# Query rotation moved to GpSimd, its root and the outputs' low halves placed elsewhere in the order

## What is computed

```python
q = rms_norm(q, q_norm); k = rms_norm(k, k_norm)
q = apply_rope(q, cos, sin)      # [t1*cos - t2*sin, t2*cos + t1*sin]
...
scores = einsum('bnqhgd,bnkhd->bnhgqk', qb, kw) * scale
m = maximum(max(scores), sink)
p = exp(scores - m)
probs = p / (sum(p) + exp(sink - m))
out = einsum('bnhgqk,bnkhd->bnqhgd', probs, vw) @ w_o
```

## Time and profile before

| | |
|---|---|
| median of 3 runs | 2738.38 us (2737.41 to 2740.35) |
| the profiled execution's own time | 2737.57 us |
| its span | 2736.3 us |
| PE busy | 2704.9 us |
| DVE, ACT, POOL busy | 1683.6, 1366.9, 0.2 us |
| mean granted clock of PE | 0.998 of full speed |
| HBM read | 491.17 MB |

### The profile page before, as it was taken

The page is one execution under the profiler, slowest core; times in us unless marked ns, Lnnn a source line. Parts: engine busy times, 40 slices in busy tenths (PEclk is TensorE's granted clock), DMA queues, the critical chain, the costliest instruction groups (busy, mean ns, idle before and its releaser), DMA issues.

```text
span 2736.3 us, 34678 instructions
## 1 busy us (share of the span) xinstructions
PE 2704.9 (99%) x13940; PEld 2297.8 (84%) x13940; DVE 1683.6 (62%) x2421; ACT 1366.9 (50%) x2032; POOL 0.2 (0%) x4
## 2 busy tenths in 40 slices
PE   8989999999999999999999999999999999999998
PEld 7768888888888888888888888888888888888886
DVE  6766566556655664565555655544568756785675
ACT  6665544344434455445444644444455535553554
POOL 0000000000000000000000000000000000000000
PEclk9999999999999999999999999999999999999999
DMA  7334666656666577668696555544556565656554
GB/s 235 116 101 154 184 188 188 198 184 193 188 195 191 181 185 198 157 150 181 188 194 221 172 184 187 191 146 157 186 178 207 182 207 179 198 184 202 185 185 146
DMA packets 256994, 495.54 MB, mean 181 GB/s; under 512 B 17201, under 2 KB 18481, under 8 KB 256322
## 3 DMA queue, kind: packets, MB, share of 16 engines
q1 hardware_dynamic: 256834, 493.33, 59.4%
HBM read 491.17 MB, written 2.10 MB: 180 GB/s over the span
## 4 chain that ended last, share of the span: by engine, by line
PE 96%; ACT 2%; DVE 1%; DMA 0%; issue 0%; SPq 0%; ACTq 0%
PE ps L446 29%; PE ps L435 16%; PE ps L437 16%; PE ps L436 16%; PE ps L451 15%; PE ps L425 1%; PE ps L517 1%; PE ps L620 1%; PE ps L681 1%; PE ps L662 1%; ACT sS L952 0%; ACT whi L862 0%; PE ps L537 0%; DMA raw<-in_attn_w_qkv 0%; PE ps L586 0%; DVE wlo L1280 0%
## 5 line engine op out<-in xcount | busy, mean ns | idle before, releaser
L862 ACT CAST whi<-raw 128x1024 fp32r<-128x1024 f32 x920 | 967.0, 1052 | 1230.8 <-PE ps L437 630.1
L1280 DVE TENSOR_TENSOR wlo<-raw,whi 128x1024 fp32r<-128x1024 f32 x920 | 1121.7, 1222 | 675.2 <-ACT whi L862 673.9
L446 PE MATMUL ps<-XA,whi 128*128 128x512 f32 x1792 | 449.1, 392 | 0.0
L446 PE MATMUL ps<-XC,whi 128*128 128x512 f32 x1664 | 416.9, 392 | 0.0
L435 PE MATMUL ps<-whi,XB 128*128 128x512 f32 x960 | 377.3, 393 | 0.0
L437 PE MATMUL ps<-whi,XB 128*128 128x512 f32 x960 | 374.1, 390 | 0.0
L436 PE MATMUL ps<-wlo,XB 128*128 128x512 f32 x960 | 373.9, 390 | 0.0
L446 PEld LDWEIGHTS ps<-XA,whi 128*128 128x128 f32 x1792 | 322.6, 189 | 57.9
L446 PEld LDWEIGHTS ps<-XC,whi 128*128 128x128 f32 x1664 | 299.5, 189 | 53.7
L435 PE MATMUL ps<-whi,XA 128*128 128x512 f32 x736 | 292.4, 397 | 0.9 <-DVE wlo L1280 0.9
L437 PE MATMUL ps<-whi,XA 128*128 128x512 f32 x736 | 287.0, 390 | 0.0
(11 more groups left out here) (227 smaller groups left out, 1889.3 us busy)
## 6 DMA issues: line engine op xcount, KB each, us to landing
raw<-in_w_up SPq DMA_DIRECT2D x176, 512.0 KB, 3.5
raw<-in_w_in SPq DMA_DIRECT2D x128, 512.0 KB, 5.1
raw<-in_ffn_w_gate SPq DMA_DIRECT2D x88, 512.0 KB, 3.5
raw<-in_ffn_w_up SPq DMA_DIRECT2D x88, 512.0 KB, 3.5
raw<-in_ffn_w_down SPq DMA_DIRECT2D x88, 512.0 KB, 4.0
raw<-in_w_down SPq DMA_DIRECT2D x88, 512.0 KB, 3.6
raw<-in_w_ckv SPq DMA_DIRECT2D x64, 512.0 KB, 4.3
raw<-in_attn_w_qkv SPq DMA_DIRECT2D x40, 512.0 KB, 3.7
```

What stands on the lines that cost most here:

```text
L446: pe.matmul(ps[:, b, :], whi[:, i, j, c], both, start=w.begin and j == 0, stop=False)
L862: act.copy(whi[:, u % NSPL, :, :], raw[:, u % NRAW, :, :]).then_inc(s.hi, 1)
L1280: dve.tensor_tensor(wlo[:, u % NSPL, :, :], raw[:, u % NRAW, :, :], whi[:, u % NSPL, :, :].bitcast(F), ALU.subtract).then_inc(s.lo, 1)
```

## The change

The rotation of the queries leaves DVE and becomes 8 instructions for each chunk on GpSimd, for both halves of the positions together. It waits for `qms` and for the tables (`rope`), no longer for the root. The root (`query_root`, ACT) stands at u+3 and no longer at u+1; the reciprocal and the two scalings (`query_scale`, DVE) stand at u+4. In DVE's loop `values` stands right behind `maxima`, ahead of `low`. PE's queue is the same, instruction for instruction.

```diff
--- before.py
+++ after.py
@@ -197,7 +197,7 @@
     x0 x1 x2 x3 pack pack2 rows_in pos poolM wpool wa wa2 ba masks mem gf out
     act dve ones xtr xhi xlo sq rms rrt rs dg wd wide res
     table sine rope mask kzero kv ksq kms krt krope ktr kT
-    qe qsq qms qrt qrs qrope qtr qT sco mx exp pn ptr pT pv bxh bx
+    qe qsq qms qswap qcos qrt qrs qrope qtr qT sco mx exp pn ptr pT pv bxh bx
     fc fsum fu fw fv silu fm hh hx fzero
     wah wal gn am aT gz lt ln ls pe pm pc pw pxh px cum bT
     gqc gs gqk ge gexp gx gp gsel gB gv sr go gsq gms grt og ogt ogh ogx sg m1 mg mT mxh mx2
@@ -1155,7 +1155,7 @@
             if c == 2:
                 act.activation(stat(6)[1][:, 0:1], stat(5)[2][:, 0:1], ACT.Sqrt)

-        q_root_at, q_turn = later(Q, 1), later(Q, 4)
+        q_root_at, q_turn = later(Q, 3), later(Q, 4)
         p_turn, p_values = later(ATTEND, 2), later(ATTEND, 3)
         wide_at, gla_root_at, gla_turn_at = later(ROOT, 2), later(GLA, 1), later(GLA, 3)
         merge_at, c_turn_at, level_exp_at = later(MERGE, 25), later(CSC, 2), later(LEVEL, 0)
@@ -1434,7 +1434,7 @@
             own.wait()
             dve.tensor_scalar(ms, ms, 1.0 / 64, EPS, ALU.mult, ALU.add).then_inc(s.qms, 1)

-        def query_first(c):
+        def query_scale(c):
             ms = sm[:, (c % 2) * 16:(c % 2) * 16 + 16]
             dve.wait_ge(s.qrt, c + 1)
             own.mark(dve.reciprocal(ms, ms))
@@ -1442,14 +1442,6 @@
             dve.tensor_scalar(ms, ms, 0.125, None, ALU.mult).then_inc(s.qrs, 1)
             dve.wait_ge(s.qrs, c + 1)
             own.mark(dve.tensor_scalar(minus[:, 32 + (c % 2) * 16:48 + (c % 2) * 16], ms, -1.0, None, ALU.mult))
-            rotate_swap(qraw[c % 2], qtmp, "q", 8, 0)
-
-        def query_second(c):
-            own.mark(rotate_sum(qraw[c % 2], qtmp, "q", 8, 0))
-
-        def query_third(c):
-            rotate_swap(qraw[c % 2], qtmp, "q", 8, 1)
-            rotate_sum(qraw[c % 2], qtmp, "q", 8, 1).then_inc(s.qrope, 1)

         def attend(n):
             c, i = divmod(n, 6)
@@ -1730,9 +1722,7 @@
                                   gf[:, c * 512:(c + 1) * 512], ALU.mult).then_inc(s.fy, 1)

         inverse_at = later(ROOT, 1)
-        q_first, p_values = later(Q, 1), later(ATTEND, 3)
-
-        q_second, q_third = ({u + n * (c > 0) + 1: c for u, c in Q.items()} for n in (1, 2))
+        q_scale, p_values = later(Q, 4), later(ATTEND, 3)
         tiles1, tiles2 = later(TILES, 1), later(TILES, 2)
         gla_norm_at, gla_turn_at = later(GLA, 1), later(GLA, 3)
         m1_at, m2_at, merge_at, c_norm_at = later(MERGE, 20), later(MERGE, 24), later(MERGE, 25), later(CSC, 1)
@@ -1741,6 +1731,8 @@
         for u in range(U_END + 1):
             if u in ATTEND:
                 maxima(ATTEND[u])
+            if u in p_values:
+                values(p_values[u])
             if u in CSC:
                 cross_max(CSC[u])
             if u == 0:
@@ -1774,18 +1766,12 @@
                 key_rotate()
             if u == 12:
                 mask_tables()
-            if u in p_values:
-                values(p_values[u])
             if u in ATTEND:
                 chances(ATTEND[u])
             if u in Q:
                 query_squares(Q[u])
-            if u in q_first:
-                query_first(q_first[u])
-            if u in q_second:
-                query_second(q_second[u])
-            if u in q_third:
-                query_third(q_third[u])
+            if u in q_scale:
+                query_scale(q_scale[u])
             if u in TILES:
                 e, ch, which, f = TILES[u]
                 tile_sum(u, e, ch, which, f)
@@ -1854,9 +1840,39 @@
             dve.tensor_scalar(o, o, stat(6)[2][:, 0:1], None, ALU.mult).then_inc(s.yd, 1)

     sync()
+
+
+    def gpsimd():
+        pool = nc.gpsimd
+
+        def query_rotation(c):
+
+            pool.wait_ge(s.rope, 1)
+            pool.wait_ge(s.qms, c + 1)
+            v = qraw[c % 2][:, :, :].rearrange("p t (h e) -> p t h e", e=64)
+            w = qtmp[:, :, :].rearrange("p t (h e) -> p t h e", e=64)
+            for t in range(2):
+                for h in range(2):
+                    b = ropeB["q"][:, t, h * 32:h * 32 + 32].unsqueeze(1).to_broadcast([P, 8, 32])
+                    e = pool.tensor_tensor(w[:, t, :, h * 32:h * 32 + 32], v[:, t, :, 32 - h * 32:64 - h * 32], b, ALU.mult)
+            e.then_inc(s.qswap, 1)
+            pool.wait_ge(s.qswap, c + 1)
+            for t in range(2):
+                a = ropeA["q"][:, t, :].unsqueeze(1).to_broadcast([P, 8, 64])
+                e = pool.tensor_tensor(v[:, t], v[:, t], a, ALU.mult)
+            e.then_inc(s.qcos, 1)
+            pool.wait_ge(s.qcos, c + 1)
+            for t in range(2):
+                e = pool.tensor_tensor(v[:, t], v[:, t], w[:, t], ALU.add)
+            e.then_inc(s.qrope, 1)
+
+        for c in range(4):
+            query_rotation(c)
+
     tensor()
     scalar()
     vector()
+    gpsimd()


 def constants():
```

## The result

The changed kernel takes 2744.77 us (median of 12 runs, 2741.56 to 2746.74) against 2737.46 before (12 runs, 2735.92 to 2740.35): ratio 1.0024, 95% interval 1.0016 to 1.0031. It is slower, by 7.3 us. The profiled execution is one of the quicker ones: 2741.84 us, span 2740.5, 4.3 us above the one of before that the prediction reads.

A forecast was written before the change was run, and what follows sets the result against it. PE bounds the kernel, busy 2704.9 of 2736.3 us, with 11.8 us of waits for DVE. Later chunks -0.9, first chunk +4.1 and clock +1.5 sum to +4.7 us: 2743.1 by the median, range 2726 to 2751.

The forecast's parts named there:

- turns: DVE and GpSimd wait for each other's SBUF reads, taking turns after each instruction; 2743.1 us by the median, chance 0.55.
- The signs that it named for the profile: GpSimd's instruction spacing, DVE's small steps a microsecond apart, PE's qraw wait, its sS and XB waits, clock below 1 near 73 us.
- three chunks win: Later three chunks: PE waits 3.5 us for probabilities and low half instead of 3.85; 0.3 us won each, 0.9 in all.
- GpSimd's price: Eight GpSimd instructions per chunk at 0.59 and 1.02 us, from the slope of ACT's cast; 6.4 us a chunk.
- the far end: GpSimd's highest price, two reads and a write at 0.81 and 1.45 us; 9.0 us a chunk, +16 us in all.
- The first chunk: Under 6 us of cover; GpSimd ends at about 73.3, PE waits 4.3 us instead of 0.2: 4.1 us lost.
- The clock: Four waits of 3.5 to 4.3 us replace three pairs; one more fall of PE's granted clock, 1.5 us.
- The rival without hindrance: GpSimd hinders nobody, so the three later chunks' waits and the clock's fall go; net -12.3 us, 2726, chance 0.30.
- The starved one: GpSimd's four products run as a burst giving DVE no turn, or cost the far price; +12 us, 2750, chance 0.15.

The follow-up runs named there:

- the memsets: Kernel before, with GpSimd doing eight memsets of 128x1024 per chunk on a scratch tile, writing but reading nothing; 2739.68 us, ratio 1.0005.
- the idle work: Kernel before, with GpSimd doing the same eight instructions per chunk on two scratch tiles, needed by nobody; 2756.19 us, ratio 1.0066.
- a better one: Changed kernel with all rotation on DVE, products in their own tile ahead of the mean squares, second half's cosine and sum at the top of u+3; 2723.04 us.
- the root's part: Kernel before with root and scalings moved, rotation on DVE not waiting for the root, low half as before; 2733.97 us, ratio 0.9985.
- the control with the late products: The 2723.04 us version on DVE, own tile kept, with its products no longer ahead of the mean squares; 2726.49 us, ratio 0.9960.

## Why the prediction was right

- **The sign and the mechanism.** Forecast: turns, 2743.1, and 2744.77 was measured. The signs that it named for the profile came: small steps stretched (their starts 0.3 to 0.7 us apart where 0.2 is usual, not a whole microsecond), a wait for qraw in the first chunk only, waits for sS and XB in the others, a granted clock below 1 behind the first chunk.
- **Turns, two-operand steps.** In the second chunk, counted from GpSimd's start, I had the maxima done at +2.4 us, the subtraction at +4.2, the scalings at +8.2, the low half at +10.1. Measured: +2.1, +3.9, +7.8, +9.5. PE waits 2.87 us, not 3.5; three chunks win 3.1 us instead of 0.9. The slopes of the earlier trace rows pointed to it, and the memsets show what it is about: reading is contended. That agrees with the Trainium skill (SBUF — State Buffer, "Who interferes with whom"), both in what excludes what and in that a GpSimd instruction which only writes blocks scalings in the doubled mode (0.53 ns an element, for 1.07 of a product) but not two-operand steps.
- **GpSimd's price.** I took 0.59 and 1.02 us from two passes at ACT's slope; alone it is 0.72 and 1.26, 7.8 us a chunk for 6.4 (the records overlap a little), between the value and the far end (9.0). The Trainium skill's scaled figure (GPSIMD Engine Reference, section 3.1), 6.7 us, is nearer, and low too. Scaled by elements, it leaves out what an instruction costs whatever its length: 0.72 and 1.26 us are 2.1 ns an element and 0.18 us besides, 1.4 us in eight instructions.
- **The first chunk, mis-sized.** Forecast +4.1 us, measured +5.9. The term was GpSimd's end at 73.3; it is 75.1. Most of it is the price (+1.4 us). The rest is the hindrance: 3.8 us (four products in 6.6 us for 2.8) where the forecast has 3.5 (1.1 until the first subtraction ends, 2.4 for two more), and small gaps. The two errors inside that 3.5 nearly cancel. GpSimd did not wait for the first subtraction to end but started at 63.41, and four subtractions ran beside it, not three: those that stood at 69.08 before, only because DVE was rotating until then, all came forward.
- **The clock.** One more fall, 1.5 us, was charged, and 1.55 measured in the profiled execution. In most executions it is probably more, by their lower mean clock (0.995 for 0.996).
- **The sum.** -0.9 + 4.1 + 1.5 = +4.7 was forecast; -3.1 + 5.9 + 1.55 = +4.35 is what the profiled execution shows (4.27 by its own time). So the sum was right partly by luck: two errors of 2 us cancelled. By the medians the difference is 7.3, and the 3 us beyond the sum are not settled; the forecast time lies only 1.7 us off because the median of before fell from 2738.38 (3 runs) to 2737.46 (12 runs). One reading is a little off and changes nothing: the last window of the earlier trace rows reaches 0.7 us past the end of the span, so 11.5 us are idle there, not 12.2.
- **The rival without hindrance** (2726) falls with the idle work. The starved one falls too: products and DVE's steps alternate, and the bursts of four don't shut DVE out.

## What to carry to other kernels

Work moved from a busy engine to an idle one is only free if the two don't shut each other out of SBUF: here each GpSimd instruction with two operands from SBUF stopped DVE's two-operand steps and scalings until it ended, and DVE was the engine with the deadline. Look first for slack in the queue that you have. With root and low half placed as in the change, the rotation's eight instructions give 2735.4 us in their old order on DVE, 2723.0 in a better one, and 2744.8 on GpSimd. Ask of each moved step which cover it has in its shortest instance (the first chunk), and of each wait removed whether what is left becomes one longer wait.

## What was not expected

- **The granted clock does not follow the length of a wait alone.** Waits of 1.35 and 2.57 us four us apart left it at 2.4 GHz in two of three chunks in the profiled execution of before. With the low half moved alone, 3.7 us in one piece took it to 1.2 GHz in all three, at 2.4, 2.7 and 1.3 us, so that 0.6 us more of waiting cost 5 us. But shorter waits did it too: 2.26 us, alone in its chunk, in all three chunks of the root's part (6.4 to 6.5 us from queries to scores for 4.91; that execution took 2735.60 us, 1.6 above its median). The pair of 1.70 and 1.17 us did it in one of three chunks with the change and in all three with the first chunk back on DVE. Waits of 1.17 us did it nowhere in the control with the late products. What decides between these cases is not shown.
- **Scalings from one operand are hindered by GpSimd's writes**, which two-operand steps are not: a pair of 128x256 takes 1.39 us for 0.62, one of 128x16 up to 0.98 for 0.17.
- **Records hide the blocking.** A blocked DVE step shows a longer duration, not idle time before it: DVE's busy time stayed at 1682.5 us (1683.6 before) though 17.7 us of rotation (4 chunks of 4.4) had left it. The mean of a group by form is the place to look.
